# Attention with rows in tiles of 128: in odd tiles ScalarE's exponential goes ahead of the copies of the turned rows, and VectorE's low parts go ahead of reciprocal, weight and output

## The reference, cut to what matters

```python
def attend(blk):
    qn, qr = blk
    s = (jnp.einsum('bqhd,bkhd->bhqk', qn, k_nope)
         + jnp.einsum('bqhd,bkd->bhqk', qr, k_rope))
    pr = jax.nn.softmax(s.astype(jnp.float32) * scale, axis=-1).astype(v.dtype)
    return jnp.einsum('bhqk,bkhd->bqhd', pr, v)
```

## Time and profile before

| what | value |
|---|---|
| median of 3 runs | 3220.55 us (3218.56 to 3220.67) |
| the profiled execution's own time | 3219.65 us |
| its span, first to last instruction | 3217.9 us |
| PE matmuls busy / PE weight loads busy | 97% / 79% of the span |
| VectorE busy | 75% of the span |
| ScalarE busy | 39% of the span |
| attention, first scores to first product of the next stage | 1205.11 to 1521.07 us, 315.96 us |

### The profile page before, as it was taken

One profiled execution on the slowest core, in us unless ns is written; L12 is line 12 of the kernel. 1 busy time (PEld: TensorE's weight loads), 2 busy tenths in 40 slices (PEclk: granted clock), 3 DMA queues, 4 the chain that ended last, 5 costly groups with the idle time before them and its releaser, 6 DMA issues.

```text
span 3217.9 us, 37930 instructions
## 1 busy us (share of the span) xinstructions
PE 3129.8 (97%) x14840; PEld 2545.9 (79%) x14840; DVE 2400.6 (75%) x4144; ACT 1240.1 (39%) x1933; POOL 2.2 (0%) x9
## 2 busy tenths in 40 slices
PE   8999999999999999988999999999999999999998
PEld 7878888877988877777878888888777687788887
DVE  6777677768869588878588767667688789789736
ACT  4333233335242455655243223223255533423414
POOL 0000000000000000000000000000000000000000
PEclk9999999999999999999999999999999999999999
DMA  3222212213433450002311111111211222122242
GB/s 128 72 79 79 72 59 73 66 59 125 123 88 126 142 191 8 7 27 90 133 53 46 59 46 53 59 46 53 66 53 52 107 74 70 40 73 93 82 170 73
DMA packets 89249, 250.68 MB, mean 78 GB/s; under 512 B 8560, under 2 KB 24304, under 8 KB 87536
## 3 DMA queue, kind: packets, MB, share of 16 engines
q1 hardware_dynamic: 89072, 248.25, 22.9%
HBM read 204.18 MB, written 44.04 MB: 77 GB/s over the span
## 4 chain that ended last, share of the span: by engine, by line
PE 87%; DVE 8%; ACT 4%; issue 1%; DMA 0%; DVEq 0%; SPq 0%; ACTq 0%
PE PS L543 85%; PE PS L548 2%; DVE WS L2167 1%; DVE X L2175 1%; DVE TMP L2167 1%; DVE X L2167 1%; ACT PT L1294 1%; DVE XS L2175 1%; ACT TMP L1772 1%; DVE COLB L2975 1%; ACT WS L1294 0%; ACT XS L1294 0%; DVE HELD L2224 0%; DVE XSf L2167 0%; DVE PT L2167 0%
## 5 line engine op out<-in xcount | busy, mean ns | idle before, releaser
L543 PE MATMUL PS<-XS,WS 128*128 128x512 f32 (+1 forms) x6480 | 1516.9, 391 | 18.1 <-DVE XS L2167 9.0
L543 PEld LDWEIGHTS PS<-XS,WS 128*128 128x128 f32 x6480 | 1210.3, 188 | 293.5 <-issue 28.8
L543 PE MATMUL PS<-HS,WS 128*128 128x512 f32 x2208 | 515.2, 393 | 13.5 <-DVE HS L2167 10.4
L543 PEld LDWEIGHTS PS<-HS,WS 128*128 128x128 f32 x2208 | 416.9, 189 | 105.3 <-DVE HS L2167 11.2
L1294 ACT ACTIVATE WS<-RAW 128x512 fp32r<-128x512 f32 (+1 forms) x390 | 305.1, 788 | 448.6 <-PE PS L543 393.2
L2167 DVE TENSOR_TENSOR WS<-RAW,WS 128x512 fp32r<-128x512 f32 (+1 forms) x390 | 344.5, 892 | 158.8 <-ACT WS L1294 157.9
L2167 DVE TENSOR_TENSOR X<-PS,X 128x512 f32<-128x512 f32 x272 | 184.4, 689 | 116.1 <-PE PS L543 116.0
L2167 DVE TENSOR_TENSOR TMP<-TMP,PS 128x512 f32<-128x512 f32 x304 | 203.7, 683 | 65.5 <-PE PS L543 59.3
L543 PE MATMUL PS<-T,WS 128*128 128x512 f32 x960 | 230.6, 389 | 0.0
L543 PEld LDWEIGHTS PS<-T,WS 128*128 128x128 f32 x960 | 180.2, 188 | 37.4
L1294 ACT ACTIVATE TMP<-PS 128x512 f32<-128x512 f32 x144 | 85.1, 595 | 306.0 <-PE PS L543 302.3
(11 more groups left out here) (334 smaller groups left out, 3643.4 us busy)
## 6 DMA issues: line engine op xcount, KB each, us to landing
RAW<-in_W SPq DMA_DIRECT2D x258, 512.0 KB, 3.4
RAWX<-in_W SPq DMA_DIRECT2D x35, 512.0 KB, 3.3
DC<-TMP SPq DMA_DIRECT2D x32, 256.0 KB, 2.1
X<-in_xT SPq DMA_DIRECT2D x8, 512.0 KB, 9.4
DX<-X SPq DMA_DIRECT2D x2, 2048.0 KB, 8.5
DCZ<-CA SPq DMA_DIRECT2D x8, 512.0 KB, 4.1
DGA<-TMP SPq DMA_DIRECT2D x16, 256.0 KB, 2.1
DGB<-TMP SPq DMA_DIRECT2D x16, 256.0 KB, 3.2
```

The lines of the kernel that those rows point to most:

```text
L543: done = d.matmul(out, l, r, start=first, stop=last)
```

## The change

It edits three of the loops. The numbers of instructions and their shapes stay as they are.

- ScalarE: in odd n, `exps(n - 1)` moves ahead of `turn_out(n - 2)`, and `o_out` behind both. Even n keeps the order `turn_out`, `exps`.
- VectorE: in every n, `turn_out(n - 2)` moves ahead of `normal(n - 2)`, and in odd n `o_out` goes behind both.
- PE: `heads_v(1, 0)` moves from the end of step 34 to the end of step 35, where the other three stand.

```diff
@@ tensor(), attention()
-                if n in (34, 35):
-                    for q in ((0,), (1, 2, 3))[n - 34]:
+                if n == 35:
+                    for q in range(4):
                         heads_v(1, q)
@@ scalar(), attention()
             for n in range(67):
+                if n % 2 == 1 and n < 65:
+                    exps(n - 1)
+                if 2 <= n < 66:
+                    turn_out(n - 2)
                 if n >= 5 and n % 2 == 1:
                     o_out((n - 5) // 2)
-                if 2 <= n < 66:
-                    turn_out(n - 2)
-                if 1 <= n < 65:
+                if 1 <= n < 65 and n % 2 == 0:
                     exps(n - 1)
@@ vector(), attention()
                 if 1 <= n < 65:
                     row_max(n - 1)
+                if 2 <= n < 66:
+                    turn_out(n - 2)
+                    normal(n - 2)
                 if n >= 5 and n % 2 == 1:
                     o_out((n - 5) // 2)
-                if 2 <= n < 66:
-                    normal(n - 2)
-                    turn_out(n - 2)
```

## The result

The changed kernel runs in 3253.33 us (median of 5, 3250.12 to 3254.18) against 3220.55 us before (median of 5). The ratio is 1.0099, 95% interval 1.0085 to 1.0113: it is slower by 33 us. The forecast was slower, 3246 us with a range of 3232 to 3260.

A forecast was written before the change was run, and what follows sets the result against it. VectorE with the exponential in its path becomes the bound; 19.0 (26 pairs) + 0 (heads_v pair) + 0.7 (first pair) + 5.6 (last head) + 1.0 (clock) = 26.3 us on 3219.65: forecast 3246 us, own range 3238 to 3256, stated range 3232 to 3260.

The forecast's parts named there:

- VectorE's loop with the exponential in it: Attention: VectorE's low parts of odd tiles wait 1.76 us for copies behind the exponential, which makes VectorE the bound.
- The loop's length: Plain pair of tiles, without queries or keys: 7.86 - 1.17 + 1.76 = 8.45 us, 0.59 us more.
- The 26 pairs with the head's extra work: Values 0 to 27 without the heads_v pair: 0.73 us more each, 19.0 us in all; a head takes 39.6 us.
- are within the 36.2 and 37.2: Heads: copies and bank waits of head_q and pair_k lie within the measured head lengths and do not bind longer.
- The pair with heads_v: Pair where PE waits for the ring's banks: from 1 us less to 1 us more, taken as 0.
- The last head: Values 27 to 31: 33.0 us against 27.4 measured before, so 5.6 us more.
- the weight's later place costs nothing: VectorE's weight behind the low parts: no cost, since values reading it stand behind the even tile's transposes and scores.
- The first pairs: First pair of the attention, tiles 0 and 1: 0.7 us more, as any other.
- The clock: PE gaps bringing stretches at 1.2 GHz: 1 us net, bounds 0 and 14 us.
- The rule on the DRAIN: VectorE: next instruction waits until the pipe empties; no overlap would cost 30 us over the attention; given no chance.
- faster: Rival: the earlier exponential closes PE's commonest gap, gaining 10.7 us, 3209 us; chance 0.05.
- Only the plain pairs: Rival: PE's work hides the new wait beside head_q or pair_k; just 10 pairs pay, 9 us, 3229; chance 0.10.

The follow-up runs named there:

- dve_only: The changed kernel with ScalarE's order of before; VectorE's new order and the moved values group stay: 3224.90 us, ratio 1.0015.
- dup_before: The kernel before with two added VectorE row maxima of the identity behind each odd tile's weight, written to unused columns: 3228.21 us, ratio 1.0022.
- ring: The changed kernel with ScalarE's and VectorE's order of before in steps n = 11, 27 and 43 alone: 3244.79 us, ratio 1.0076.
- tail: The changed kernel with ScalarE's and VectorE's order of before from n = 64 on: 3250.82 us, ratio 1.0095.
- act_only: The changed kernel with VectorE's order of before; ScalarE's new order and the moved values group stay: 3282.05 us, ratio 1.0189.
- dup_after: The changed kernel with two added VectorE row maxima of the identity behind each odd tile's weight, written to unused columns: 3266.42 us, ratio 1.0143.

## Why the prediction was right, and what it missed

- **VectorE's loop with the exponential in it: shown.** The new wait was put at 1.76 us and is 1.76. Taking the exponential out of it (`dve_only`), shortening the loop by 0.40 us and lengthening it by 0.39 each moved the plain pair as the theory says. The signs named beforehand came as well: the wait for the copies at 61.7 us (some 50 named), the transposes' wait for low parts at 32.9 (20 or more), the plain pair at 8.57 (8.4 to 8.6). One reading beside it was wrong: before the change VectorE did not have "1.17 us to spare". `dup_before` shows some 0.2 us.
- **The loop's length** was put at 8.45 us and is 8.57. The missing 0.12 us is the output's start: 0.32 us behind the weight's (1510.15 to 1510.47), where other work follows it after 0.20 (1513.96 to 1514.16).
- **The 26 pairs with the head's extra work**: 19.0 us forecast, 21.0 measured. Near, but by an account that was partly wrong. The step that failed is the sentence that PE's bank waits "are within the 36.2 and 37.2": `pair_k` waits for the output of the same step, which the change put last, behind the wait for the copies. `ring` puts a price of 8.5 us on those three steps; in it the 26 pairs are only 13.9 us longer than before. So the loop's share was put about 3 us too high (13.9 and the 2 us named there, against 19.0) and the bank wait at nothing, and that the two nearly cancel is luck. Heads took 40.5 and 42.0 us where 39.6 was forecast.
- **The pair with heads_v**: 0 forecast, -0.5 measured. The move alone shortens it by 3.2 us and the new orders take most of that back, with a bank wait of 2.51 us that the prediction did not have.
- **The last head**: 5.6 forecast, 7.1 measured, and the way from the last values to the next stage 1.4 us longer where nothing was forecast. The sentence that "the weight's later place costs nothing" failed for tile 63, where no transposes and scores stand between it and the values: PE waited 1.97 us. `tail` got 2.5 us back.
- **The first pairs**: 0.7 forecast, 1.7 measured.
- **The clock**: 1 us net forecast. The mean granted clock of the attention fell from 0.97 to 0.95, and the start of the next stage ran at 0.50 (1.2 GHz). In the attention PE was busy 7.7 us longer for the same 1747 matmuls (287.68 and 295.40). How much of that is time can't be read apart from the slack, but for one place. From the last `values` to the next stage the engines' work is one chain; at 0.50 PE's two pieces took 4.83 us, where they had taken 3.40 at 1.00 with a wait of 0.64 between them, and that is the 1.4 us of the last head's bullet. Behind the attention the span grew by 1.2 us. The 2.3 us ahead of the attention has nothing to do with the change: the two runs of the values group alone are the same program, and reach the first scores at 1205.0 and 1207.5 us.
- **The rule on the DRAIN**: the prediction says that the trace disagrees with the Trainium skill. The same section (VectorE: DVE Perf Modes, The DRAIN you can't avoid) adds that a next instruction starts earlier when it is not held back. The start 0.08 us before the end in the earlier trace rows agrees with that. The sum went by the measured starts and is not touched.
- **The rivals**: "faster" falls with `act_only`. "Only the plain pairs" was wrong, since pairs with queries and keys paid more in all, not less. It held for one pair in four: those with the first `head_q` (ending at values 3, 7, 11, 15, 19 and 23) kept their 9.21 us. But that saved nothing. Through the head from values 7 to 11 VectorE waits for ScalarE alone, four times 1.76 us among that, and `dup_after` made this head 1.54 us longer, four times 0.39. What the one pair hides the next ones pay.
- **The whole**: 26.3 us forecast, 32.8 measured.

## What to carry to other kernels

When an instruction is moved ahead on one engine, follow the other engine's order through the same step: if it produces what the moved one waits for and then itself waits for what the moved one now delays, the two engines run in turn, and each pair of steps costs the sum. Idle time on an engine is not slack; the slack is the time between its result and the one who needs it, which was 0.2 us here where VectorE idled 1.17. And where buffers come from a ring, list who waits for the buffer that the moved step frees: three such places of 67 steps carried a quarter of the loss.

## What was not expected of the hardware

The lower clock reached across the end of the attention. PE waited there for 1.97 us and then 2.85 us, and from 1546.60 to 1559.70 the granted clock was 0.50 (1.2 of 2.4 GHz), although PE was busy for 10.25 of the 13.1 us. The first twelve matmuls of the next stage took 5.46 us. In the kernel before, PE waited the same 2.85 us at this place with waits of 0.73 and 0.64 us ahead of it, the clock was 1.00 behind it, and the same twelve took 2.96 us. With the old order in the last steps (`tail`) it was 0.68. `dve_only`, `ring` and `dup_after` have the late weight too, with the same wait of 1.97 us. In these three and the changed kernel the way from the last `values` to the next stage takes 6.94 to 7.68 us, 6.25 in the kernel before and in `tail`. So in four kernels the late weight of one tile went with 0.7 to 1.4 us beyond its own wait. The clock of the next stage does not hang on that wait alone: its first 2 us ran at 0.50 in those four, but also at 0.77 in `tail` and at 0.57 in `dup_before`, whose weights are not late.
